# Seven block products in all four up projections, the modulation's matrix products in other places, and four waits

## What is computed

```python
def conv_ffn(xn, w_up, conv_w, conv_b, w_down):          # first block, both layers ("a0", "a1")
    h = causal_depthwise_conv(xn @ w_up, conv_w) + conv_b
    g, u = jnp.split(h, 2, axis=-1)
    return (jax.nn.gelu(g) * u) @ w_down

def layer(x, xc, silu_c, silu_cc, lp, ...):              # second block, both layers ("b0", "b1")
    mod = (silu_c @ lp["w_mod"] + lp["b_mod"])[:, None, :]        # 6 * 1024 numbers
    ...                                                           # for the context: modc, in layer 0 all six
    h = modulate(x, lp["g_norm1"], sh1, sc1)                      # parts, in layer 1 only the first two
    ...
    x = x + gt1 * merge_branches(o_mla, o_gqa, o_four, proj[..., GATE_START:], lp)
    x = x + gt2 * conv_ffn_2(modulate(x, lp["g_norm2"], sh2, sc2), lp)
```

## Time and profile before

| | |
|---|---|
| runs | 2662.96, 2663.04, 2668.32 us |
| profiled execution | 2663.28 us, its span 2661.5 us |
| PE busy | 2583.9 us (97%) |
| PE weight load busy | 1996.5 us (75%) |
| DVE busy | 1110.0 us (42%) |
| ACT busy | 534.9 us (20%) |
| POOL busy | 470.2 us (18%) |
| DMA | 334.00 MB, mean 125 GB/s |

### The profile page before, as it was taken

One profiled execution on the slowest core, in us unless ns is written; L12 is line 12 of the kernel. 1 busy time (PEld: TensorE's weight loads), 2 busy tenths in 40 slices (PEclk: granted clock), 3 DMA queues, 4 the chain that ended last, 5 costly groups with the idle time before them and its releaser, 6 DMA issues.

```text
span 2661.5 us, 31643 instructions
## 1 busy us (share of the span) xinstructions
PE 2583.9 (97%) x12174; PEld 1996.5 (75%) x12174; DVE 1110.0 (42%) x2106; ACT 534.9 (20%) x1109; POOL 470.2 (18%) x408
## 2 busy tenths in 40 slices
PE   7999999999889999999999999999999999999999
PEld 5757888886677888845566766888846865898997
DVE  3024167741312878223552223565500335434860
ACT  1122132111202221102440002222200124212220
POOL 0011111000101111001342211333200004332530
PEclk9989999999999999999899999999999998999999
DMA  5422277743224776211002222122211220243442
GB/s 202 158 95 83 107 284 270 290 150 127 105 101 174 268 276 249 91 66 48 1 24 72 95 79 95 64 95 95 105 57 75 75 101 1 103 167 127 158 182 103
DMA packets 32558, 334.00 MB, mean 125 GB/s; under 512 B 3008, under 2 KB 9280, under 8 KB 9280
## 3 DMA queue, kind: packets, MB, share of 16 engines
q1 hardware_dynamic: 32448, 332.45, 33.3%
HBM read 331.39 MB, written 1.05 MB: 125 GB/s over the span
## 4 chain that ended last, share of the span: by engine, by line
PE 89%; DVE 5%; issue 2%; POOL 2%; DMA 1%; ACT 1%; DVEq 0%; ACTq 0%; POOLq 0%
PE PS L552 26%; PE PS L660 12%; PE PS L860 11%; PE PS L2480 6%; PE PS L1577 5%; PE PS L1418 5%; PE PS L2521 4%; PE PS L1236 3%; PE PS L1589 2%; PE PS L2057 2%; PE PS L1247 2%; PE PS L1259 2%; PE PS L430 1%; DMA slot<-in_weights 1%; PE PS L842 1%
## 5 line engine op out<-in xcount | busy, mean ns | idle before, releaser
L552 PE MATMUL PS<-arena,slot 128*128 128x256 f32 x1824 | 400.1, 382 | 9.9 <-POOL arena L1978 5.6
L552 PEld LDWEIGHTS PS<-arena,slot 128*128 128x128 f32 x1824 | 348.9, 192 | 60.1 <-POOL arena L1978 6.6
L552 PE MATMUL PS<-XN,slot 128*128 128x256 f32 (+1 forms) x1248 | 312.4, 411 | 5.0 <-DVE XN L492 5.0
L660 PE MATMUL PS<-XN,slot 128*128 128x256 f32 x1408 | 306.3, 381 | 5.1 <-DVE XN L492 5.1
L660 PEld LDWEIGHTS PS<-XN,slot 128*128 128x128 f32 x1408 | 268.8, 191 | 42.7 <-issue 5.9
L552 PEld LDWEIGHTS PS<-XN,slot 128*128 128x128 f32 x1248 | 237.8, 191 | 76.7 <-issue 43.0
L860 PE MATMUL PS<-SQ,slot 128*128 128x256 f32 (+1 forms) x992 | 173.0, 327 | 0.0
L860 PEld LDWEIGHTS PS<-SQ,slot 128*128 128x128 f32 x992 | 152.2, 191 | 12.9
L860 PE MATMUL PS<-XN,slot 128*128 128x256 f32 (+1 forms) x832 | 148.0, 328 | 0.0
L1577 PE MATMUL PS<-arena,slot 128*128 128x512 f32 x328 | 141.1, 592 | 0.0
L860 PEld LDWEIGHTS PS<-XN,slot 128*128 128x128 f32 x832 | 128.6, 191 | 11.6
(11 more groups left out here) (248 smaller groups left out, 3323.0 us busy)
## 6 DMA issues: line engine op xcount, KB each, us to landing
slot<-in_weights SPq DMA_DIRECT2D x86, 2048.0 KB, 7.7
arena<-in_mod SPq DMA_DIRECT2D x48, 1024.0 KB, 6.8
slot<-in_weights SPq DMA_DIRECT2D x16, 2816.0 KB, 9.9
slot<-in_weights SPq DMA_DIRECT2D x24, 1536.0 KB, 6.6
slot<-in_weights SPq DMA_DIRECT2D x2, 2176.0 KB, 8.7
slot<-in_weights SPq DMA_DIRECT2D x4, 1024.0 KB, 4.8
small<-in_small SPq DMA_DIRECT2D x1, 2685.0 KB, 19.0
arena<-in_c SPq DMA_DIRECT2D x2, 1024.0 KB, 10.3
```

The source lines that it names most:

```text
L552: mm = pe.matmul(o, l, r, start=k == 0, stop=k == len(terms) - 1, skip_group_check=True)
L660: mm = pe.matmul(o, slots[slot][:, a:a + P], XN[:, k, seg[g]], start=k == 0, stop=k == DK - 1, skip_group_check=True)
```

## The change

It does six things.

1. `upa0` and `upa1` use the seven block products (with `TSUM_A`, a layout of the token sums that leaves the other half of SQ alone); `tensor_up` and its companions are gone. The direct pair 0 runs in two halves of the tokens, in b1 too.
2. In all four up stages `c21` and `c22` go to PSUM bank 7 in place of `CU`, and the weight sum s2 moves from DVE to POOL.
3. Modulation tiles are loaded and multiplied one by one (0.5 MB), and spread: of layer 0, 24 tiles are in a0 and 24 in a1 (five in the up stage, 19 beside the down projection); the 48 of layer 1 are in `merge0` (steps 3 to 11: four tiles in each of four steps, then seven, seven, six, six, six). There the first 16 take two products each, the others one. Half of a step's tiles stand after `c21`, half between the two `gated`. Their ring has two slots.
4. `memkv0` starts from memory scaled by the gain alone and multiplies the keys by the reciprocal root when it reads them out; its norm's sum comes after the first job.
5. The gates of `lstm` alternate between two groups of output partitions (0 to 3 and 32 to 35), and the value tokens of `lstmin` use banks 6, 7, 0 and 1 in place of 0 to 3, which the convolution still reads.
6. `wo1` and its norm run in halves of 128 tokens, as `wo0` does with 256.

```diff
+        tiles += g[0::2] + g[1::2] + u[0::2] + u[1::2]
...
+        MODP = H[:, DK:DK + 4, T:2 * T]
+        mod_slots = [area(15360 + D * i, 4, T) for i in range(4)]
+        LATEC, LATEP = area(8192, 2, D), area(12288, D)
+        late_slots = [area(10240 + D * i, D) for i in range(2)]
...
+        def vector_mod_turn(dve, s, g, turn):
+
+            f = int(s[1])
+            if g == 0:
+                sem, landed = mod_landed(f, 0)
+                dve.wait_ge(sem, landed + 16 * turn)
+                dve.wait_ge(*of(s, "mod_kept", turn=turn, back=1))
+            w = mod_slots[0]
+            vector_mod_product(dve, w, MODC[:, g, :, :], tiny[:, 48 + g:49 + g], w if g else MODP)\
+                .then_inc(*tick(MD, s, "mod_product", g))
+            if g:
+                dve.wait_ge(*of(s, "mod_product", 1, turn=turn))
+                dve.tensor_copy(MOD[:, 0, bass.ds(turn + MOD_HALF * f, 1), :],
+                                tiny[:, 48:50].rearrange("p (m g) -> p m g", g=2)).then_inc(*tick(MD, s, "mod_kept"))
+
+        def vector_mod_tile(dve, s, r, g):
+            f = int(s[1])
+            w = mod_slots[mod_slot(r)]
...
+        def vector_mod_tile(dve, s, r, g):
+            f = int(s[1])
+            w = mod_slots[mod_slot(r)]
+            if g == 0:
+                dve.wait_ge(*mod_landed(f, r))
+                if r > MOD_LOOP:
+                    dve.wait_ge(*of(s, "mod_tile", r - 1, 0))
+            vector_mod_product(dve, w, MODC[:, g, :, :], MOD[:, 0, MOD_HALF * f + r, g:g + 1], w if g else MODP)\
+                .then_inc(*tick(VD, s, "mod_tile", r, g))
+
...
+        LATE = {u: [] for u in range(12)}
+        for q in range(MOD_TILES):
+            LATE[3 + q // 4 if q < 16 else 7 + (q - 16) // 7 if q < 30 else 9 + (q - 30) // 6].append(q)
+
+        def vector_late_tile(dve, q):
+
+            w = late_slots[q % 2]
+            dve.wait_ge(sems[f"late_landed{q % 2}"], 16 * (q // 2 + 1))
+            for g in range(2 if q < 16 else 1):
+                if q < 16 and g == 0 and q:
+                    dve.wait_ge(*of("late_product", q - 1, 0))
+                vector_mod_product(dve, w, LATEC[:, g, :], MOD[:, 1, q, g:g + 1], LATEP if q < 16 and g == 0 else w)\
+                    .then_inc(*tick(VD, "late_product", q, g))
+            C.found[("late", q)] = C.found[("late_product", q, 1 if q < 16 else 0)]
...
+                for g in range(2):
...
+                            c = slice(g * h, (g + 1) * h)
+                            mm = pe.matmul(PS[:, 7 * half, c], slots[slot][:, a:a + P], XN[:, k, c],
                                            start=k == 0, stop=k == DK - 1, skip_group_check=True)
...
-            first = turn is None and i == 1
-            return [PS[:, (i - 1) % 2, 0:n], PS[:, 7, 0:n] if first else CU[:, 0:n]]
+            return [PS[:, (i - 1) % 2, 0:n], PS[:, 7, 0:n]]
...
-                dve.wait_ge(*w_of(s, "s1", i, turn))
-                dve.wait_ge(*w_of(s, "s3", i, turn))
-                dve.tensor_tensor(s2, s1, a11, ALU.subtract).then_inc(*w_tick(s, VD, "s2", i, turn))
...
-                dve.tensor_tensor(CU[:, h:n], PS[:, 2 + i % 2, 0:h], U3[:, 0:h], ALU.add)\
+                dve.tensor_tensor(PS[:, 7, h:n], PS[:, 2 + i % 2, 0:h], U3[:, 0:h], ALU.add)\
...
-                dve.tensor_tensor(CU[:, 0:h], U3[:, 0:h], PS[:, 6, 0:h], ALU.subtract)\
+                dve.tensor_tensor(PS[:, 7, 0:h], U3[:, 0:h], PS[:, 6, 0:h], ALU.subtract)\
                     .then_inc(*w_tick(s, VD, "c21", i, turn))
+                if s[0] == "a" and turn is not None:
+                    if i == 0:
+                        dve.wait_ge(*of(s, "silu_c"))
+                    if i % 2 == 0:
+                        vector_mod_turn(dve, s, i // 2, turn)
+                elif s[0] == "a" and i >= W_LAST and i % 2 == 0:
+                    vector_mod_tile(dve, s, MOD_LOOP, (i - W_LAST) // 2)
...
+                pool.wait_ge(*w_of(s, "s1", i, turn))
+                pool.tensor_tensor(s2, s1, a11, ALU.subtract).then_inc(*w_tick(s, GD, "s2", i, turn))
...
+                add(vector=lambda d: [vector_mod_tile(d, s, r, g) for r in range(5, 11) for g in range(2)])
...
+                    for r in (range(11, 15), range(15, 22), range(22, MOD_HALF), ())[j]:
+                        for g in range(2):
+                            vector_mod_tile(dve, mod, r, g)
+                    if j == 2:
+                        vector_mod_end(dve, 0, int(mod[1]), [(mod, "mod_tile", MOD_HALF - 1, 1)])
...
+                MEMG, MEMR = area(12288, DK, T), area(14336, T)
+
+                def vector_mem_gain(dve):
+                    dve.wait_ge(sems["loaded_mem"], 16)
+                    for m in range(DK):
+                        dve.tensor_scalar(MEMG[:, m, :], MEM[:, m, :], col("mem_norm0", m), None, ALU.mult)\
+                            .then_inc(*tick(VD, "memnorm", "gain", m))
+
+                def vector_mem_rstd(dve):
+                    dve.wait_ge(*of("memnorm", "rstd", 0))
+                    dve.tensor_copy(MEMR, RT[:, 0, 0:T]).then_inc(*tick(VD, "memnorm", "rstd_kept"))
+                    dve.wait_ge(*of("memnorm", "rstd_kept"))
+
+                def mem_keys_read(j, bank, i):
+                    return lambda e: e.tensor_tensor(KM[0][:, 2 * j + i, :], PS[:, bank, i * T:(i + 1) * T], MEMR, ALU.mult)
                 jobs = feature_jobs(
-                    lambda k: MEMN[0][:, k, :], lambda k, s=s: (s, "out", 0, k), 8,
-                    lambda j, bank: [("vector", copy_op(KM[0][:, 2 * j:2 * j + 2, :], copies(None, bank)))])
-                jobs[1]["then"] = lambda pe, mixnorm=mixnorm: tensor_norm(pe, "mixnorm0", mixnorm)
...
+                jobs[0]["then"] = lambda pe, un=un: tensor_norm(pe, "memnorm", [un])
+                jobs[2]["then"] = lambda pe, mixnorm=mixnorm: tensor_norm(pe, "mixnorm0", mixnorm)
+                add(tensor=lambda pe, jobs=jobs: tensor_linear(pe, "memkv0", jobs))
+                add(vector=vector_mem_gain)
+                add(scalar=lambda a, un=un: scalar_norm(a, "memnorm", [un]), vector=lambda d, un=un: vector_norm(d, "memnorm", [un]),
+                    gpsimd=lambda p, un=un: gpsimd_norm(p, "memnorm", [un]))
+                add(vector=vector_mem_rstd)
+                add(vector=lambda d, jobs=jobs: reads_linear(d, VD, "vector", "memkv0", jobs[:3]))
...
+                def tensor_lstm_gates(pe, lw=lw):
+                    claim(pe, 4)
+                    for k in range(DK):
+                        pe.wait_ge(*of("mixnorm1", "out", 0, k))
+                        for i in range(2):
+                            mm = pe.matmul(PS[32 * i:32 * i + 4, 4, 0:T], lw[:, k, 4 * i:4 * i + 4], xn(k), start=k == 0,
+                                           stop=k == DK - 1, skip_group_check=True)
...
+                add_tokens("lstmin", lambda k, t: XN[:, k, t * P:(t + 1) * P], 2, DK, 2, 6,
+                           [V1[:, t, h * 512:(h + 1) * 512] for h in range(2) for t in range(2)], ring=8)
...
+                    if l == 0 and u == 2:
+                        act.wait_ge(sems["loaded_c"], 16 * 3)
+                        act.activation(LATEC, LATEC, ACT.Silu).then_inc(*tick(SD, "late_silu"))
...
+                        late = LATE[u] if l == 0 else []
+                        if late and late[0] == 0:
+                            dve.wait_ge(*of("late_silu"))
+                        for q in late[0:len(late) // 2]:
+                            vector_late_tile(dve, q)
...
+                        if u and i == 0:
+                            for q in late[len(late) // 2:]:
+                                vector_late_tile(dve, q)
+                if l == 0:
+                    for n in range(2):
+                        vector_mod_end(dve, 1, n, [("late", MOD_TILES - 1)])
...
-                add_out(f"wo{l}", lambda k, n=nq: Y[:, k, 0:n], lambda k, l=l: (f"merge{l}", "merged", k), DK, segs,
-                        gate1)
-                add_norm(s, norm_x(s, X, XN, lambda m, g, l=l: GAIN[:, l, 1, m, g:g + 1],
-                                   after_out(f"wo{l}", segs, gate1), segs, shift=mod_col(l, 3)))
-                add_ffn(f"b{l}", "b", segs, lambda m, g, s=s: [(s, "out", 0, m)], gate2)
+                part = [slice(0, P), slice(P, T)]
+                norms = [[f"{s}{i}", norm_x(f"{s}{i}", X, XN, lambda m, g, l=l: GAIN[:, l, 1, m, g:g + 1],
+                                            after_out_half(f"wo{l}", i), [0], shift=mod_col(l, 3), span=(i * P, P))]
+                         for i in range(2)]
+                add_out_halves(f"wo{l}", lambda k, c: Y[:, k, c], lambda k, l=l: [(f"merge{l}", "merged", k)], DK,
+                               range(4, DK), gate1, norms, (0, DK - 1), part)
+                add_ffn(f"b{l}", "b", segs, lambda m, g, s=s: [(f"{s}{g}", "out", 0, m)], gate2)
...
+                if stage in ("upa0", "upa1") and g == first_slab[stage] + 2:
+                    f = int(s[1])
```

(52 more changed lines are left out.)

350 lines of the change are left out of this document (98 added, 252 removed).

## The result

| | before | after |
|---|---|---|
| median | 2665.62 us | 2633.85 us (2632.27 to 2636.65) |
| profiled execution, its span | 2663.28, 2661.5 us | 2636.65, 2634.9 us |

The ratio is 0.9882, 95% interval 0.9865 to 0.9899: 32 us faster by the medians, 26.6 by the two profiled executions. The forecast was 2628, its range 2610 to 2650. The time lies inside it, and 6 us above the forecast.

A forecast was written before the change was run, and what follows sets the result against it. PE was taken to bound the kernel, at 89% of the chain. Gains of 46.2 us less 11 us lost in `merge0` gave -35: 2663.3 - 35 = 2628 us, range 2610 to 2650.

The forecast's parts named there:

- Fewer columns: Up stages: a stage shortens only by fewer PE columns or where PE waits; 21 steps of 6.27 us are 131.7 us.
- a0: First up stage of the a kind: from 152.3 to 142.4 us, -9.9.
- Up in a0 and a1: Prediction's paragraph on these two stages: 131.7 us of steps plus pair 0, together 140.4, plus two possible waits.
- a rival for the slab period: Up stages a0, a1, b1: the period stays 13.3 us in all three, +18, time 2646; chance 0.15.
- The silu on ScalarE: Start of a0: ACT's silu of the vector delays the p1 copy and bias, so c22 comes late: 1 us, a0 alone.
- Slab waits: Up stages: PE waiting at the hand-over of weight slabs, put at 1 us per stage, bounds 0 and 8.
- `merge0`: Second layer's modulation tiles put into this stage: +11 us, bounds 1 and 60.
- ring: Steps with one-product tiles in two slots: DVE waits for tiles to land, between 0 and +9, taken as +4.
- lateness at the end: End of the merge, before `wo0`: the half before and the step before make DVE late by some 5: +5.
- low clock: After the wait at the end of the merge, PE runs at half speed: 2 us.
- `wo1`, start, lstm: Halved `wo1` with norm and pair 0, -6.1; PE's earlier first products, -6.1; gates and value tokens, -3.5 and -2.6.
- Both lstm terms: Gates overlapping in two column groups, -3.5 us; value tokens no longer waiting for the convolution, -2.6 us.

The follow-up runs named there:

- the second execution: The changed kernel itself, nothing altered, run again beside the last two follow-up kernels: 2633.30 us, ratio 0.9886 to the kernel before.
- the first version tried: Changed kernel with GpSimd's first three weight sums in a0 and a1 waiting for the norm's last output, VectorE's token sums ahead of its own weight sum: 2634.00 us.

## Why the prediction was right, and where it was not

- **Fewer columns.** Right: 21 steps at 6.27 us. a1 was forecast at 141.4 and is 141.3 (of the 154.8 us taken for it before, in a window that begins 0.6 us ahead of its first product, 154.2 are the stage); b1's steps 132.7 and 131.9; b0 unchanged, as forecast.
- **a0.** Forecast -9.9, measured -8.7 in the stage and +2.8 ahead of it, so -5.9. This is the step that failed. It was a term missing in the sum: "Up in a0 and a1" priced the sums of GpSimd and their slab waits in the steps, but not what they do to the norm ahead of pair 0. In a0 GpSimd had been idle there before. I had named the mechanism, the shared port, only as a rival for the slab period; the run with later sums shows its 2.8 us at the norm and 1.2 in pair 0. The rule behind it (the Trainium skill, SBUF — State Buffer, "SBUF: two separate sides") holds here with 0.43 against 1.37 us.
- **The silu on ScalarE.** Forecast 1 us in a0; measured nothing, since pair 0 ended late. The run with GpSimd's sums later shows it: 1.14 us at the copy.
- **Slab waits.** Forecast 1 us per stage. PE's waits for the sums add up to 1.6 us in a0, 0.4 in a1 and 0.3 in b1, so the term was about right. I gave the shorter period to the fast tap and to `s2` together; the runs give all of it to the tap.
- **`merge0`.** Forecast +11, split in 4 (ring), 5 (lateness at the end) and 2 (low clock). Measured +10.8: 5.7 until `wo0` begins, 3.2 of waiting in its first tile and 2.0 of low clock. A tile of 0.5 MB lands in 3.5 us (3.6 forecast), and DVE waits for tiles from step 7 on, as forecast. The mechanism is right. That the sum fits to 0.2 us is luck: the same stretch cost 6.4 to 10.8 us in eight executions, and this one is the highest.
- **`wo1`, start, lstm.** Forecast -6.1, -6.1, -6.1; measured -5.4, -6.3, -6.1. The start was only read from the traces, no run isolates it: PE's first product was forecast at 12.3 and came at 12.24. Both lstm terms were undone one by one: 3.5 us (3.5 forecast) and 2.7 (2.6).
- **The modulation in the down projections.** Forecast 0; their stretches are unchanged to 0.1 us.
- **The remaining 4.8 us** (+1.5, +1.8, +1.5) are in attentions that the change does not touch, and in no term. They go with the granted clock: 0.86 before and 0.84 after in the fox attention, 0.95 and 0.93 between the lstm's value tokens and up a1 (0.95 again, and 226.3 us, in the second execution), and in the second block the decay alone grew by 3.3 us at 0.65 and 0.51 (last section).

The forecast sum was -35; the traces give -26.6. The difference is 2.8 + 1.2 in a0, 4.8 of clock, 0.7 in `wo1` and 0.6 in a1 (the window above), less 1.5 in the other rows.

## What to carry over

A stretch whose work fits can still cost: count the round trip of a tile against the number of slots, step by step, not busy time alone. Here 24 MB and 87 us of products in a merge were free with four slots and an even spread, and cost 6.4 to 10.8 us with two slots and an uneven one. When an engine gets new work, look at what it now meets ahead of the stage, not only inside it. And a removed wait may be cover for the next one: of 4.0 us freed in a0, 2.4 went back in the steps of the first version tried.
